# A seven-slot weight ring for the first request, and the row turns of the second attention: one encoder layer on one Trainium2 core

## What is computed

```
h = rms_norm(x);  proj = h @ w_in                       # 2048 x 10240: q, k, v of mixers A and B, two gates
oa = dilated_window_attention(qa, ka, va)               # 12 heads in 3 groups, merged by log-sum-exp to 4
ob = grouped_query_attention(qb, kb, vb)                # 8 query heads, 2 key/value heads, all 256 keys
x = x + (sigmoid(ga) * (oa @ w_br_a) + sigmoid(gb) * (ob @ w_br_b)) @ w_out
h = rms_norm(x);  q = h @ w_pq;  s = q @ sub_keys       # 8 heads, 2 x 128 keys
e, g = top 16 of the 16 x 16 best sums, softmax         # 128 experts of 16384 for each token
x = x + sum_k  g_k * gelu(u_emb[e_k] . h) * v_emb[e_k]
```

## Time and profile before

| | |
|---|---|
| three runs | 3879.2, 3882.32, 3889.35 us |
| profiled execution: its own time | 3878.53 us |
| its span, first to last instruction | 3876.7 us |
| PE, DVE, ACT, POOL busy | 91%, 80%, 37%, 17% of the span |
| DMA | 1103.45 MB, mean 285 GB/s |
| mean granted TensorE clock | 0.938 |

### The profile page before, as it was taken

One profiled execution on the slowest core, in us unless ns is written; L12 is line 12 of the kernel. 1 busy time (PEld: TensorE's weight loads), 2 busy tenths in 40 slices (PEclk: granted clock), 3 DMA queues, 4 the chain that ended last, 5 costly groups with the idle time before them and its releaser, 6 DMA issues.

```text
span 3876.7 us, 48449 instructions
## 1 busy us (share of the span) xinstructions
PE 3547.1 (91%) x19308; PEld 3047.6 (79%) x19310; DVE 3091.8 (80%) x3731; ACT 1443.9 (37%) x1999; POOL 668.1 (17%) x516
## 2 busy tenths in 40 slices
PE   7997888999789999899868999999989999999997
PEld 5875555777668887677868999977779999997775
DVE  3664676878678987887875889988888998989986
ACT  4554656554332223233222123344421333334443
POOL 0000000001112421421000012233310222223331
PEclk9999999999889999899889589999985999999999
DMA  5651887677569999987333069999970999999997
GB/s 183 188 174 55 291 284 239 207 236 277 190 238 386 394 392 352 374 310 270 109 93 120 1 275 408 409 384 384 387 290 28 415 414 372 415 407 380 394 379 277
DMA packets 288704, 1103.45 MB, mean 285 GB/s; under 512 B 24928, under 2 KB 25312, under 8 KB 219104
## 3 DMA queue, kind: packets, MB, share of 16 engines
q1 hardware_dynamic: 208928, 530.64, 39.2%
q0 software_dynamic: 73728, 536.90, 34.5%
q10 hardware_dynamic: 5824, 32.80, 2.1%
HBM read 1089.77 MB, written 10.49 MB: 284 GB/s over the span
## 4 chain that ended last, share of the span: by engine, by line
PE 62%; DVE 19%; DMA 11%; ACT 4%; issue 2%; PEld 1%; ACTq 0%; POOL 0%; DVEq 0%; PEldq 0%
PE ps L1308 26%; PE ps L1544 15%; PE ps L1598 8%; PE ps L1527 5%; DVE w_lo L828 5%; PE ps L1573 4%; DMA w<-v_emb 4%; ACT w_hi L447 3%; DVE acc L853 2%; DVE rows L845 2%; DMA w<-w_in 2%; DMA w<-w_out 1%; DMA rows<-v_emb,eidx 1%; DMA w<-u_emb 1%; DMA w<-w_pq 1%
## 5 line engine op out<-in xcount | busy, mean ns | idle before, releaser
L447 ACT ACTIVATE w_hi<-w 128x1024 fp32r<-128x1024 f32 x752 | 796.7, 1060 | 1286.4 <-PE ps L1308 713.2
L828 DVE TENSOR_TENSOR w_lo<-w,w_hi 128x1024 fp32r<-128x1024 f32 x752 | 918.7, 1223 | 437.3 <-ACT w_hi L447 432.0
L1308 PE MATMUL ps<-w_hi,ht_all 128*128 128x512 f32 x3328 | 843.6, 398 | 25.3 <-ACT w_hi L447 25.0
L1308 PEld LDWEIGHTS ps<-w_hi,ht_all 128*128 128x128 f32 x3328 | 630.6, 192 | 170.6 <-ACT w_hi L447 22.9
L429 POOL DMA_INDIRECT rows<-u_emb,eidx x256 | 333.7, 1304 | 1882.3 <-DVE dots L845 1044.0
L853 DVE SCALAR_TENSOR_TENSOR acc<-rows,coef,acc 128x2048 f32<-128x2048 f32 x256 | 600.8, 2347 | 7.7 <-DMA rows<-v_emb,eidx 6.5
L845 DVE CUSTOM_DVE_ANT_0 rows<-rows,h 128x2048 f32<-128x2048 f32 x256 | 584.6, 2284 | 0.4 <-issue 0.2
L1544 PE MATMUL ps<-ht_all,w_hi 128*128 128x256 f32 x4096 | 554.3, 288 | 2.9 <-ACT w_hi L755 2.9
L429 POOL DMA_INDIRECT rows<-v_emb,eidx x256 | 334.2, 1305 | 1273.3 <-DVE acc L853 1220.8
L1544 PEld LDWEIGHTS ps<-ht_all,w_hi 128*128 128x128 f32 x4096 | 508.4, 191 | 3.6 <-issue 3.1
L1308 PE MATMUL ps<-w_lo,ht_all 128*128 128x512 f32 x1664 | 453.3, 398 | 36.4 <-DVE w_lo L828 34.6
(11 more groups left out here) (191 smaller groups left out, 2959.7 us busy)
## 6 DMA issues: line engine op xcount, KB each, us to landing
w<-w_in SPq DMA_DIRECT2D x320, 512.0 KB, 4.5
w<-u_emb SPq DMA_DIRECT2D x256, 512.0 KB, 9.7
w<-v_emb SPq DMA_DIRECT2D x256, 512.0 KB, 7.9
w<-w_out SPq DMA_DIRECT2D x64, 512.0 KB, 6.4
w<-w_pq SPq DMA_DIRECT2D x64, 512.0 KB, 5.7
w<-w_br_b SPq DMA_DIRECT2D x32, 512.0 KB, 5.9
w<-w_br_a SPq DMA_DIRECT2D x16, 512.0 KB, 7.2
x_src<-x ACTq DMA_DIRECT2D x3, 2048.0 KB, 9.5
```

The costliest lines, as they stand in the source:

```text
L447: act.activation(w_hi[:, g % 2, :, :], w[:, g % RING, :, :], ACT.Copy).then_inc(hi_ready, 1)
L828: dve.tensor_tensor(w_lo[:, g % 2, :, :], w[:, g % RING, :, :], w_hi[:, g % 2, :, :].bitcast(F32), ALU.subtract).then_inc(lo_ready, 1)
L1308: ins = pe.matmul(ps[:, seg.bank + t, :], lhs(t)[:, half, k, :], wt[:, g % 2, kk, :], start=(j == 0 and part == 0 and kk == 0), stop=(j == ...
```

## The change

It has three parts.

1. **The ring.** `w` has 7 slots (`WIDE_RING`) up to the end of the second `qkv` and 4 from the first slab of the second `mix` (`NARROW_G0`, slab 344). `plan_ring` lists slot, use and the slab that had the slot before; `load`, `hi`, `lo` and the U stages go by these lists. SP waits for `lo` of the slab that had the slot before, seven slabs earlier instead of four.
2. **Room for it.** `w` begins 12 KB lower. `sq` (now 8 rows, used twice over, with a wait on `squared` from the third group on) and `junk2` move behind `w_lo`; the first top-k's tables move to where `raw` tiles 8 and 9 lie, so ScalarE waits for `topk_done` at tile 8 instead of tile 10.
3. **The second attention.** `maxima(1)` stands ahead of the loop and `maxima(u + 2)` behind the scaling of `u` and `rest(u - 1)`; the norm and the turns come after it. `ATT_TURNS` has four turns, at units 1, 3, 5 and 7.

```diff
-RING = 4
+RING, WIDE_RING = 4, 7
-ATT_TURNS = (0, 1, 1, 1, 0, 1, 1, 0, 1, 1, 0, 1, 1, 0, 1, 0)
+NARROW_G0 = STAGES[1]["mix"][0].g0
+ATT_TURNS = (0, 1, 0, 1, 0, 1, 0, 1, 0, 0, 0, 0, 0, 0, 0, 0)
+def plan_ring():
+    slot, number, prior, at_slot = [], [], [], {}
+    for g in range(W_SLABS + 4 * HB * HALVES):
+        s = g % WIDE_RING if g < NARROW_G0 else WIDE_RING - RING + (g - NARROW_G0) % RING
+        slot.append(s)
+        number.append(at_slot[s][0] + 1 if s in at_slot else 1)
+        prior.append(at_slot[s][1] if s in at_slot else None)
+        at_slot[s] = (number[-1], g)
+    return slot, number, prior
...
-    sq = ab("sq", 112, [16, DH], BF16)
-    w = at("w", R_W, [RING, SK, CT], F32)
+    sq = at("sq", R_F + 16 * K, [8, DH], BF16)
+    w = at("w", R_W, [WIDE_RING, SK, CT], F32)
...
-                need(sp, lo_ready, g - RING + 1)
-                sp.dma_start(w[:, g % RING, :, :], src).then_inc(w_loaded[g % RING], 16)
+                if SLOT_PRIOR[g] is not None:
+                    sp.wait_ge(lo_ready, SLOT_PRIOR[g] + 1)
+                sp.dma_start(w[:, SLOT[g], :, :], src).then_inc(w_loaded[SLOT[g]], 16)
...
-                    if p == 1 and seg.ct == 10:
+                    if p == 1 and seg.ct == 8:
                         act.wait_ge(topk_done, 1)
...
+                    if j >= 2:
+                        act.wait_ge(squared, SQUARES * p + 4 * k + j - 1)
...
                 maxima(0)
+                maxima(1)
                 for u in range(N_UNITS):
-                    if u + 1 < N_UNITS:
-                        maxima(u + 1)
                     dve.wait_ge(exp_done, N_UNITS * r + u + 1)
...
                     if u:
                         rest(u - 1)
+                    if u + 2 < N_UNITS:
+                        maxima(u + 2)
                     if r == 1:
```

More of the change, by code:

```diff
@@ L194, in plan_turns @@
     return quota, ends, rest
+SLOT, SLOT_USE, SLOT_PRIOR = plan_ring()
 QUOTA, TURN_ENDS, TURNS_LEFT = plan_turns()
@@ L247, in encoder @@
     R = o
-    R_W, R_F, R_ACC0 = R + 116 * K, R + 132 * K, R + 150 * K + 512
+    R_W, R_F, R_ACC0 = R + 104 * K, R + 132 * K, R + 150 * K + 512
     R_ROWS = R_ACC0 + 8 * K
@@ L280, in encoder @@
               lambda t: h2_23[:, t, :] if t < 2 else h2_1[:, :]]
-    junk = [ab("junk0", 72, [D]), ab("junk1", 16, [D]), ab("junk2", 104, [CT]), ab("junk3", 76, [D], BF16), ab("junk4", 104, [CT])]
+    junk = [ab("junk0", 72, [D]), ab("junk1", 16, [D]), at("junk2", R_F + 16 * K, [CT], F32), ab("junk3", 76, [D], BF16), ab("junk4", 104, [CT])]
     h_turned = [ht_all, ht_all, mt0, ht_all, ht_all]
@@ L298, in topk_places @@
     def topk_places(p):
-        cand_kb, kb = ((72, 104), (64, 96))[p]
+        cand_kb, kb = ((72, 64), (64, 96))[p]
         b = R + kb * K
@@ L328, in encoder @@
     sk_in, y_out = S("sk_in"), S("y_out")
-    w_loaded = [S(f"w_loaded{j}") for j in range(RING)]
+    w_loaded = [S(f"w_loaded{j}") for j in range(WIDE_RING)]
     hi_ready, lo_ready, slab_done = S("hi_ready"), S("lo_ready"), S("slab_done")
@@ L416, in _ @@
                     for j in range(2 * HB):
-                        need(sp, lo_ready, g0 + j - RING + 1)
-                        sp.dma_start(w[:, (g0 + j) % RING, :, :].rearrange("p k c -> p (k c)"),
-                                     blocks[HB * h + j // 2, :, D // 2 * (j % 2):D // 2 * (j % 2 + 1)]).then_inc(w_loaded[(g0 + j) % RING], 16)
+                        sp.wait_ge(lo_ready, SLOT_PRIOR[g0 + j] + 1)
+                        sp.dma_start(w[:, SLOT[g0 + j], :, :].rearrange("p k c -> p (k c)"),
+                                     blocks[HB * h + j // 2, :, D // 2 * (j % 2):D // 2 * (j % 2 + 1)]).then_inc(w_loaded[SLOT[g0 + j]], 16)
         @block.gpsimd
@@ L444, in hi @@
             def hi(g):
-                act.wait_ge(w_loaded[g % RING], 16 * (g // RING + 1))
+                act.wait_ge(w_loaded[SLOT[g]], 16 * SLOT_USE[g])
                 need(act, slab_done, g - 1)
-                act.activation(w_hi[:, g % 2, :, :], w[:, g % RING, :, :], ACT.Copy).then_inc(hi_ready, 1)
+                act.activation(w_hi[:, g % 2, :, :], w[:, SLOT[g], :, :], ACT.Copy).then_inc(hi_ready, 1)
             def turn_split(gr, dst):
@@ L507, in squares @@
                         for h in range(4):
-                            ins = act.activation(sq[:, 4 * j + h, :], raw[:, 2 * k + c, t, h * DH:(h + 1) * DH],
+                            ins = act.activation(sq[:, 4 * (j % 2) + h, :], raw[:, 2 * k + c, t, h * DH:(h + 1) * DH],
                                                  ACT.Square, accum_out=ss[:, 4 * j + h:4 * j + h + 1])
@@ L827, in lo @@
                 dve.wait_ge(hi_ready, g + 1)
-                dve.tensor_tensor(w_lo[:, g % 2, :, :], w[:, g % RING, :, :], w_hi[:, g % 2, :, :].bitcast(F32),
+                dve.tensor_tensor(w_lo[:, g % 2, :, :], w[:, SLOT[g], :, :], w_hi[:, g % 2, :, :].bitcast(F32),
                                   ALU.subtract).then_inc(lo_ready, 1)
@@ L1523, in turn_block @@
                 def turn_block(g):
-                    pe.wait_ge(w_loaded[g % RING], 16 * (g // RING + 1))
+                    pe.wait_ge(w_loaded[SLOT[g]], 16 * SLOT_USE[g])
                     pe.wait_ge(lo_ready, g - 1)
@@ L1527, in turn_block @@
                         ins = pe.transpose(ps[:, 2 * (g % 2) + k // 4, k % 4 * P:(k % 4 + 1) * P],
-                                           w[:, g % RING, k // 4, k % 4 * P:(k % 4 + 1) * P], ident[:, :])
+                                           w[:, SLOT[g], k // 4, k % 4 * P:(k % 4 + 1) * P], ident[:, :])
                     ins.then_inc(u_turned, 1)
```

## The result

The changed kernel takes 3831.66 us (median of four runs, 3824.97 to 3834.48) against 3882.69 us (four runs of the kernel before, three of them those known at the forecast). The ratio is 0.9864, 95% interval 0.9845 to 0.9883: 51 us or 1.4% faster. Forecast were 3836 us and a gain of 46 us.

A forecast was written before the change was run, and what follows sets the result against it. The ring's four slots, not the DMA engines, were taken to pace request 0's 152 slabs, and turns to lengthen `attention(1)`. Terms -28 - 6 - 2 + 1 - 13 + 2 = -46 gave 3836 us beside the median, range 3816 to 3865.

The forecast's parts named there:

- `mix` and `out`: -28: In request 0, seven slots no longer bind and the `w_hi` pair sets the pace: 239 to 210 us, -28.
- `pq`: -6: In request 0, the same gain per slab would be 7.5 us; as it begins with a full ring, -6.
- Second `qkv`: -2: Two landing waits of 2.8 us in all go away with more slots: -2 us, bounds 0 and 2.8.
- Start: +1: Three more early loads slow the last constants: +1 us, 0 to 1.9 by sharing, 8 at most by issue order.
- `attention(1)`: -13: Seven uncovered turns go, four ahead of a scaling cost 7 us: 91.8 to 78.5 us, -13, bounds -7 and -25.
- half of the clock loss kept: In `attention(1)`, 8.6 us were put down to the slow clock; 4.3 us of that were to stay.
- Tail: +2: Three turns behind the last add cost 6.8 us, but the last write then runs alone: +2 us, or +6.
- `attention(0)` and the stages put at 0: VectorE's rows in `attention(0)` are unchanged, 0; three turns in the V stage, 0, at most 7 us.
- that the engines bind: Rival: DMA engines limit `mix` and `out` once the ring does not; sum -19, 3863 us; chance 0.17.
- deeper queues: Rival: seven outstanding loads slow each other in request 0; slower, 3907 us at 250 GB/s; chance 0.04.
- the turns hold the scaling: Rival: `attention(1)` keeps the slow clock and shows every turn, gaining 7 us or nothing; 3842 to 3849 us; chance 0.08.
- The clock case: Rival: clock and waits come back in full, -41 for the ring, -25 for `attention(1)`; 3817 us; chance 0.06.

The follow-up runs named there:

- experiment 4: Changed kernel, but SP waits for all small constants ahead of the first weight load; 3826.06 us, ratio 0.9855.
- experiment 7: Changed kernel with `ATT_TURNS` all 0, so seven turns are left behind the last add; 3838.37 us, ratio 0.9884.
- experiment 8: Changed kernel with the ten turns of before, each right behind the scaling, ahead of `rest` and the maxima; 3829.29 us, ratio 0.9869.
- experiment 1: Changed kernel with its seven slots, but VectorE's loop and the ten turns of the kernel before; 3848.16 us, ratio 0.9916.

## Why the prediction was right

*`mix` and `out`: -28, measured -28.0.* The slot's cycle is shown as the cause: with the attention left as it was, the gain stays (208.7 us), with four slots it is gone (237.4), and landing waits vanish although a landing takes no less. The pace that was read from two undisturbed slabs, 3.19 us, is the pace of the stage now (3.20). That ScalarE's other 18 us would all show held too: 211.1 us against 210, with 64.8 us of idle time ahead of 120 `hi`, 0.54 each, which is the 1.60 of the pace less the 1.06 of a `hi`. What the step left out is the spread of landings; the cycle of 7.2 us, made with the median landing, would have let five slots pass as enough, and they give two thirds.

*`pq`: -6, measured -6.6. Second `qkv`: -2, measured -0.3* from first to last `hi` (294.3 to 294.0): its landing waits are gone, but slabs 272 to 282 took 1.6 us longer at a granted clock of 0.91, not 1.00.

*Start: +1, measured +1.5*, inside the bound of 1.9 that followed from sharing and far from the 8 of issue order; experiment 4 shows the sharing from the other side. The Trainium skill ("DMA: Bandwidth & Descriptors", Queues, rings and completion order) has each DMA engine take the queues in turn, packet by packet; the 1.5 us agree with it.

*`attention(1)`: -13, measured -19.1, the term that was mis-sized.* Its parts can now be measured one by one. The norm was put at 3.3: 3.2. Four turns ahead of a scaling were put at 7, 1.7 each: 6.1, 1.5 each. The forecast's own rows give 4.2 - 2.9 = 1.3 each, 5 in all, so the 1.7 did not follow from them; the measured price lies between the two. Without norm and turns, 63.3 us are left, against 63.9 assumed. The step that failed is "half of the clock loss kept", 4.3 us: next to nothing of it was kept. Granted clock in the changed kernel is 0.91, with no turns 0.92, in `attention(0)` 0.92 before; TensorE was busy 2.0 us longer than without turns (49.15 against 47.12), and that is counted in the 6.1.

The loss itself was put too low. Without turns `attention(1)` takes 91.8 - 66.6 = 25.2 us less than with the ten of before. In the forecast's terms that is seven uncovered turns at 2.28 (16.0) and 9.2 left over for the clock (8.6 there), a split by subtraction. The windows of before and of experiment 7 split it otherwise: TensorE was busy 60.98 us and 47.12, 13.9 more for the same 224 instructions at the slower clock, and stood idle 32.0 us and 20.7, 11.3 more.

In experiment 8 ten turns leave the clock at 0.92, so it does not go with the number of turns. There TensorE has four waits of over 2 us between the first and the last transposes, 2.1 to 3.0 us long; in the kernel before it has eight, 2.1 to 5.8. The Trainium skill ("TensorE: Matmul & The Clock Gate", HAM oscillation) has a TensorE that waits between short bursts start the next one at half its clock; the 0.92 with four such waits and the 0.76 with eight agree, and the forecast's term of -18 by that rule was the better one. The waits are not all of it: experiment 1 has the same eight and a clock of 0.82.

*Tail: +2, measured +2.7* from the end of the last add to the end of the span (9.46 to 12.18). The turns there are those with `v_emb`, 2.35 us each and not 2.28, and VectorE waited 0.7 us between: 7.9 us to the write instead of 6.8.

*`attention(0)` and the stages put at 0.* T of `attention(0)` is 64.6 (63.9 before); in thirteen kernels with the same rows there it goes from 62.2 to 67.9; the granted clock was 0.95 where it took 62.2 and 0.88 where it took 67.3. Behind `attention(1)` the profiled execution gained 5.6 us up to the last add, which no step named. These stages differ by as much between kernels whose code there is the same (367 to 382 us in the last V stage), and the median gained 51.0 us, the profile 53.5: I take them for no part of the change, though only the spread speaks for it.

By the steps measured here, 1.5 - 28.0 - 6.6 - 0.3 - 19.1 + 2.7 = -49.8, near the 51.0 of the medians. It leaves out the stretch from the first `hi` to that of `mix` (first `qkv` and `attention(0)`), which was put at 0 and took 1.8 us longer (351.3 to 353.1), and the 5.6 us behind `attention(1)`; with both it is the profile's 53.5, but for rounding. Of the forecast's own terms two errors mattered, -6 in `attention(1)` and +1.7 in the second `qkv`, and the range took in both. That they and the stages put at 0 partly cancel is luck. Of the rivals, that the engines bind falls with the 321 GB/s at a share of 0.91, 353 at a full one, above the 338 of before; deeper queues did not slow the rate, either. That the turns hold the scaling did happen, at about the forecast's own price (6.1 us for 7). The clock case was half right: the clock came back, the rest did not shrink further.

## What to carry to other kernels

When loads are late though the DMA engines are not full, add up a slot's cycle (issue, landing, use, release) and divide by the slots; then take the slow landings, not the median, to choose their number. Put filler work on an engine into the wait that it has anyway, ahead of the instruction that would wait, and never between a result and the one that TensorE waits for: here ten turns cost 1.4 us in one place and 20 to 25 in the others. Where TensorE waits often, count the slow clock as part of the wait's price (here 13.9 of 25.2 us); in this kernel it came back with the waits.

## What the runs showed of the hardware that was not expected

The slow clock cost as much as the waits that came with it. In `attention(1)` the same 224 TensorE instructions were busy 61.0 us at a granted clock of 0.76, 55.7 at 0.82, 49.2 at 0.91 and 47.1 at 0.92. The kernel before and that of experiment 1, with the same instructions in the same order there, differ by 4.9 us in T through it alone, as far as the rows show: TensorE stood idle 32.0 and 32.6 us of the two windows. The difference lies at the start, 11.5 us at a granted clock of 0.55 in the one and 1.00 in the other; behind them it is 0.79 and 0.80. Why it fell earlier in the one stays open.

```profile
1005.50:1017.00 11.50, 9.44 (x30) 7.47 (x31) 5.86 (x13) 3.89 (x8) 0.94 (x1) 0.55 0.19 56
1017.00:1098.50 81.50, 51.53 (x195) 40.03 (x193) 47.15 (x97) 28.78 (x70) 8.50 (x9) 0.79 0.38 134
```

and in experiment 1:

```profile
975.20:986.70 11.50, 8.89 (x48) 7.37 (x48) 6.56 (x15) 5.11 (x10) 0.94 (x1) 1.00 0.28 91
986.70:1063.40 76.70, 46.77 (x176) 36.57 (x176) 46.43 (x96) 27.59 (x67) 8.50 (x9) 0.80 0.38 137
```

At the start the DMA engines moved 407 GB/s at a full share (4 to 14 us in the changed kernel) with the input, the constants and the weights under way, so that what is not needed yet holds up what is: four or seven early slab loads moved the first work from 14.4 to 19.9 or 21.4 us.
